# A long convolution inside a three-branch block: the real parts on VectorE, splits between the products, a place of its own for the odd frequencies

## The reference

```python
def fft_conv(u, cf):
    L = u.shape[1]
    U = jnp.fft.rfft(u.astype(jnp.float32), n=2 * L, axis=1)
    y = jnp.fft.irfft(U * cf[None], n=2 * L, axis=1)[:, :L]
    return y.astype(u.dtype)

z = x1 * (fft_conv(v, cf[:, 0]) + hy_d[0] * v)
z = x2 * (fft_conv(z, cf[:, 1]) + hy_d[1] * z)
```

## Time and profile before

| what | value |
|---|---|
| median of 3 runs | 1131.82 us |
| profiled execution | 1131.72 us |
| span of its trace | 1130.0 us |
| PE busy | 1078.3 us, 95% of the span |
| DVE busy | 726.5 us, 64% |
| ACT busy | 539.4 us, 48% |
| POOL busy | 74.9 us, 7% |

### The profile page before, as it was taken

The page is one execution under the profiler, slowest core; times in us unless marked ns, Lnnn a source line. Parts: engine busy times, 40 slices in busy tenths (PEclk is TensorE's granted clock), DMA queues, the critical chain, the costliest instruction groups (busy, mean ns, idle before and its releaser), DMA issues.

```text
span 1130.0 us, 14634 instructions
## 1 busy us (share of the span) xinstructions
PE 1078.3 (95%) x4942; PEld 869.9 (77%) x4942; DVE 726.5 (64%) x1187; ACT 539.4 (48%) x828; POOL 74.9 (7%) x70
## 2 busy tenths in 40 slices
PE   5999999999999999999999998899899999999998
PEld 4777678888887878788888777677577877888887
DVE  2865875554557987755455677987938676545553
ACT  3654454444445555644444462545346545444442
POOL 5013000000000100000000002201500000000000
PEclk9999999999999999999999999998899999999999
DMA  9454255656555534565655552443234445555553
GB/s 243 136 170 137 76 162 185 194 187 186 186 186 169 169 129 130 174 193 187 187 188 186 168 153 89 147 134 112 93 129 132 150 160 173 188 186 186 186 186 112
DMA packets 133599, 182.04 MB, mean 161 GB/s; under 512 B 11446, under 2 KB 80322, under 8 KB 133490
## 3 DMA queue, kind: packets, MB, share of 16 engines
q1 hardware_dynamic: 132266, 178.40, 50.2%
q0 software_dynamic: 1056, 2.57, 1.1%
q10 hardware_dynamic: 232, 0.49, 0.1%
HBM read 180.36 MB, written 1.05 MB: 161 GB/s over the span
## 4 chain that ended last, share of the span: by engine, by line
PE 75%; DVE 16%; ACT 5%; issue 2%; DMA 1%; SPq 1%; POOL 0%; DVEq 0%; ACTq 0%; POOLq 0%
PE ps L1788 14%; PE ps L1799 14%; PE ps L1791 14%; PE ps L1809 6%; PE ps L1810 6%; PE ps L1814 6%; DVE wlo L1042 5%; PE ps L1773 2%; PE ps L1775 2%; PE ps L1774 2%; DMA raw<-in_a_w_in 1%; PE ps L1879 1%; ACT whi L581 1%; PE ps L1862 1%; PE ps L2001 1%
## 5 line engine op out<-in xcount | busy, mean ns | idle before, releaser
L1042 DVE TENSOR_TENSOR wlo<-raw,whi 128x1024 fp32r<-128x1024 f32 x338 | 410.9, 1247 | 154.6 <-ACT whi L581 154.0
L581 ACT ACTIVATE whi<-raw 128x1024 fp32r<-128x1024 f32 x338 | 342.1, 1053 | 115.6 <-DMA raw<-in_a_w_in 28.1
L1788 PE MATMUL ps<-whi,ath 128*128 128x512 f32 (+1 forms) x896 | 360.7, 403 | 7.0 <-DVE atl L1056 4.8
L1791 PE MATMUL ps<-whi,atl 128*128 128x512 f32 (+1 forms) x896 | 351.8, 393 | 0.0
L1799 PE MATMUL ps<-wlo,ath 128*128 128x512 f32 (+1 forms) x896 | 243.0, 393 | 5.9 <-DVE wlo L1042 5.9
L1788 PEld LDWEIGHTS ps<-whi,ath 128*128 128x128 f32 x896 | 170.7, 191 | 51.9 <-issue 10.3
L1799 PEld LDWEIGHTS ps<-wlo,ath 128*128 128x128 f32 x896 | 168.7, 190 | 42.8 <-DVE wlo L1042 7.6
L1791 PEld LDWEIGHTS ps<-whi,atl 128*128 128x128 f32 x896 | 170.8, 191 | 33.6 <-issue 0.5
L1809 PE MATMUL ps<-whi,brh 128*128 128x512 f32 x272 | 106.5, 392 | 0.4 <-issue 0.4
L1810 PE MATMUL ps<-whi,brl 128*128 128x512 f32 x272 | 105.9, 389 | 0.0
L1118 DVE TENSOR_TENSOR brl<-ps,brh 128x512 fp32r<-128x512 f32 x33 | 22.8, 692 | 95.8 <-ACT brh L627 95.8
(11 more groups left out here) (338 smaller groups left out, 1043.8 us busy)
## 6 DMA issues: line engine op xcount, KB each, us to landing
raw<-in_ffn_w_in SPq DMA_DIRECT2D x176, 256.0 KB, 3.0
raw<-in_ffn_w SPq DMA_DIRECT2D x132, 256.0 KB, 2.9
raw<-in_w_in SPq DMA_DIRECT2D x104, 256.0 KB, 2.9
raw<-in_ffn_w_out SPq DMA_DIRECT2D x88, 256.0 KB, 2.8
raw<-in_a_w_in SPq DMA_DIRECT2D x48, 256.0 KB, 3.4
raw<-in_b_w_in SPq DMA_DIRECT2D x48, 256.0 KB, 3.1
raw<-in_a_w_out SPq DMA_DIRECT2D x16, 256.0 KB, 2.9
raw<-in_b_w_out SPq DMA_DIRECT2D x16, 256.0 KB, 2.9
```

The source lines that it names most:

```text
L581: a_(unit_view(whi, slot, w), unit_view(raw, slot, w), ACT.Copy).then_inc(hi_ready, 1)
L1042: v_.tensor_tensor(unit_view(wlo, slot, w), unit_view(raw, slot, w), unit_view(whi, slot, w), ALU.subtract).then_inc(lo_ready, 1)
L1788: mm(ps[bk + t][:, 0:w], ath[:, k, t * P:(t + 1) * P], rh[:, kk, :], start=k == 0, stop=False)
L1791: mm(ps[bk + t][:, 0:w], atl[:, k, t * P:(t + 1) * P], rh[:, kk, :], start=False, stop=False)
```

## The change

The real parts are made by DVE, in spectral_end, beside the imaginary ones, and POOL has no part in the round. The second pair of products gets a function of its own, spectral_imag, and one unit split stands ahead of it and one behind it, where two stood ahead of both. forward(o) signals after each pair of products, ACT copies the odd half of each pair as soon as that pair is signalled, and puts it in h_o, which overlaps no tile that is in use in the two rounds. DVE folds the first pair when its copy is there. The semaphore counts follow.

```diff
--- before.py
+++ after.py
@@ -307,6 +307,7 @@
         C_th = W(7680, 2048).rearrange("p (t n) -> p t n", t=NT)
         h_u = W(7680, 2048).rearrange("p (i n) -> p i n", i=4)
         C_mg = W(9728, 2048).rearrange("p (t n) -> p t n", t=NT)
+        h_o = W(11776, 1024).rearrange("p (i n) -> p i n", i=2)
         h_w = W(9728, 2048).rearrange("p (i n) -> p i n", i=4)
         C_qT = W(11776, 1024).rearrange("p (h t) -> p h t", h=4)
         C_kT = W(12800, 512).rearrange("p (h t) -> p h t", h=2)
@@ -508,17 +509,6 @@
                     nc.gpsimd.tensor_tensor(y, y, B_T1[:, kind, t, :].unsqueeze(1).to_broadcast([P, 4, BD]),
                                             ALU.mult).then_inc(sem("b_scaled"), 1)
 
-
-            def hyena_sums(o):
-
-                pool.wait_ge(sem("h_prod"), 6 * o + 2)
-                nc.gpsimd.tensor_tensor(h_w[:, 0:2, :], h_w[:, 0:2, :], h_w[:, 2:4, :], ALU.subtract).then_inc(sem("h_y"), 1)
-                pool.wait_ge(sem("h_y"), 3 * o + 1)
-                nc.gpsimd.tensor_tensor(h_w[:, 2, :], h_w[:, 0, :], h_w[:, 1, :], ALU.add).then_inc(sem("h_y"), 1)
-                nc.gpsimd.tensor_tensor(h_w[:, 3, :], h_w[:, 0, :], h_w[:, 1, :], ALU.subtract).then_inc(sem("h_y"), 1)
-
-            hyena_sums(0)
-            hyena_sums(1)
 
             pool.wait_ge(evac_act, ACT_EVACS[18])
             pool.wait_ge(sem("c_ssq"), 5)
@@ -860,9 +850,9 @@
 
             def h_odd(o):
 
-                act.wait_ge(sem("h_fwd"), o + 1)
                 for kind in range(2):
-                    a_(C_vt[:, kind, :], ps[5 + 2 * kind][:, :], ACT.Copy).then_inc(sem("h_odd"), 1)
+                    act.wait_ge(sem("h_fwd"), 2 * o + kind + 1)
+                    a_(h_o[:, kind, :], ps[5 + 2 * kind][:, :], ACT.Copy).then_inc(sem("h_odd"), 1)
 
             def c_squares(pieces):
 
@@ -1543,23 +1533,34 @@
 
             def spectral(o):
 
-                dve.wait_ge(sem("h_odd"), 2 * o + 2)
-                ec, oc, es, os = ps[4][:, :], C_vt[:, 0, :], ps[6][:, :], C_vt[:, 1, :]
-                for i, (a, b, op) in enumerate(((ec, oc, ALU.add), (ec, oc, ALU.subtract), (es, os, ALU.add), (os, es, ALU.subtract))):
-                    v_.tensor_tensor(h_u[:, i, :], a, b, op).then_inc(sem("h_folded"), 1)
+                for kind in range(2):
+                    dve.wait_ge(sem("h_odd"), 2 * o + kind + 1)
+                    even, odd = ps[4 + 2 * kind][:, :], h_o[:, kind, :]
+                    v_.tensor_tensor(h_u[:, 2 * kind, :], even, odd, ALU.add).then_inc(sem("h_folded"), 1)
+                    if kind == 0:
+                        v_.tensor_tensor(h_u[:, 1, :], even, odd, ALU.subtract).then_inc(sem("h_folded"), 1)
+                    else:
+                        v_.tensor_tensor(h_u[:, 3, :], odd, even, ALU.subtract).then_inc(sem("h_folded"), 1)
                 dve.wait_ge(sem("h_folded"), 4 * o + 4)
                 v_.tensor_tensor(h_w[:, 0:2, :], h_u[:, 0:2, :], H[:, o, 0:2, :], ALU.mult).then_inc(sem("h_prod"), 1)
                 v_.tensor_tensor(h_w[:, 2:4, :], h_u[:, 2:4, :], H[:, o, 2:4, :], ALU.mult).then_inc(sem("h_prod"), 1)
 
-            def spectral_end(o):
+            def spectral_imag(o):
 
                 dve.wait_ge(sem("h_prod"), 6 * o + 2)
                 v_.tensor_tensor(h_u[:, 0:2, :], h_u[:, 0:2, :], H[:, o, 2:4, :], ALU.mult).then_inc(sem("h_prod"), 1)
                 v_.tensor_tensor(h_u[:, 2:4, :], h_u[:, 2:4, :], H[:, o, 0:2, :], ALU.mult).then_inc(sem("h_prod"), 1)
+
+            def spectral_end(o):
+
                 dve.wait_ge(sem("h_prod"), 6 * o + 4)
-                link(v_.tensor_tensor(h_u[:, 0:2, :], h_u[:, 0:2, :], h_u[:, 2:4, :], ALU.add))
+                v_.tensor_tensor(h_w[:, 0:2, :], h_w[:, 0:2, :], h_w[:, 2:4, :], ALU.subtract).then_inc(sem("h_parts"), 1)
+                v_.tensor_tensor(h_u[:, 0:2, :], h_u[:, 0:2, :], h_u[:, 2:4, :], ALU.add).then_inc(sem("h_parts"), 1)
+                dve.wait_ge(sem("h_parts"), 2 * o + 2)
+                v_.tensor_tensor(h_w[:, 2, :], h_w[:, 0, :], h_w[:, 1, :], ALU.add).then_inc(sem("h_prod"), 1)
+                v_.tensor_tensor(h_w[:, 3, :], h_w[:, 0, :], h_w[:, 1, :], ALU.subtract).then_inc(sem("h_y"), 1)
                 v_.tensor_tensor(h_u[:, 2, :], h_u[:, 0, :], h_u[:, 1, :], ALU.subtract).then_inc(sem("h_prod"), 1)
-                v_.tensor_tensor(h_u[:, 3, :], h_u[:, 0, :], h_u[:, 1, :], ALU.add).then_inc(sem("h_prod"), 1)
+                v_.tensor_tensor(h_u[:, 3, :], h_u[:, 0, :], h_u[:, 1, :], ALU.add).then_inc(sem("h_y"), 1)
 
             def hyena_gate(o):
                 for m in range(4):
@@ -1578,6 +1579,8 @@
             h_taps(0)
             feed(U_C + 11)
             spectral(0)
+            feed(U_C + 12)
+            spectral_imag(0)
             feed(U_C + 13)
             spectral_end(0)
             feed(U_C + 15)
@@ -1586,6 +1589,8 @@
             hyena_gate(0)
             feed(U_C + 20)
             spectral(1)
+            feed(U_C + 21)
+            spectral_imag(1)
             feed(U_C + 22)
             spectral_end(1)
             feed(U_C + 24)
@@ -2241,11 +2246,13 @@
                 pe.wait_ge(sem("h_tok"), NT * (o + 1))
                 for i in range(4):
                     ins = mm(ps[4 + i][:, :], fwd[:, i, :], C_vt[:, i % 2, :], start=True, stop=True)
+                    if i == 1:
+                        ins.then_inc(sem("h_fwd"), 1)
                 ins.then_inc(sem("h_fwd"), 1)
 
             def backward(o):
 
-                pe.wait_ge(sem("h_y"), 3 * o + 3)
+                pe.wait_ge(sem("h_y"), 2 * o + 2)
                 pe.wait_ge(sem("h_prod"), 6 * o + 6)
                 for m in range(4):
                     for q in range(2):
```

## The result

The changed kernel takes 1125.78 us (median of 5 runs, 1122.50 to 1126.87) against 1133.38 us (5 runs, 1130.24 to 1134.98): ratio 0.9928, 95% interval 0.9905 to 0.9951. The forecast was 1124.3 us, 0.7% faster. The profiled execution took 1125.78 us.

What follows compares the result with a forecast made beforehand. Bound: PE waiting for DVE, itself held by POOL, and half clock. PE's 4.85 us lead after round 0, plus 0.5 and 2.05 in round 1, gives 7.4 (7.5 by schedule): 1131.82 to 1124.3 us, range 1122.6 to 1126.0.

Steps and rivals of the forecast that it cites:

- Folds earlier in round 0: Odd frequencies' own place, one count per pair: round 0's folds end 1.75 us earlier; round 1 gains 0.5 us.
- Less DVE a round: Each round DVE loses 4.4 us of POOL contention and gains 2.35 us of real parts: net 2.05 us less.
- Order of the splits: In each round, weight splits placed between the products: priced at 0, bounds -0.2 to +0.1 us.
- Round 0's wait gone, full clock behind it: Before round 0's backward transform PE's 3.16 us wait goes, 0.9 us in hand; full clock gives 1.7 us.
- Rival 1: Clock not given back in the backward transform, or a later wait newly loses its clock: 1126.0 us; chance 0.14.
- What is late next: Round 1's backward turn needs DVE's gate, ending about 693.8; PE arrives at 694.4, clear by 0.6 us.
- Unit 20 and unit 22: PE's waits for low weight parts in round 1: about 0.6 of 0.75 us goes; 2.8 of 4.88 us remain.
- Rival 2: Round 1's gain eaten by a late high part or DMA: 1127 to 1128.6 us; chance 0.06.
- Rival 3: DVE's slow rate comes from operands, not POOL, so its added work comes on top: 1134.1 us; chance 0.05.
- Clock later on: Clock behind the remaining wait for unit 22 and later waits: kept at 0, bounds -1.7 to +1.7 us.
- Rival 4: The stretch behind 763 also runs at full clock: 1122.6 us; chance 0.05.
- Does it last?: From 749.50 on, waits hang on PE, DVE and ACT alone, so the whole rest moves by 7.5 us.

Runs made afterwards that it cites:

- e4: Changed kernel with POOL also doing its old three instructions on memory nobody needs, no instruction of the two rounds waiting for them; ratio 1.0006.
- e5: Changed kernel with POOL starting three memsets, which only write, at the point of its old work; 1127.0 us in one run, ratio not timed.
- e3: Changed kernel with both weight splits of each round put back ahead of the imaginary products; 1124.62 us, ratio 0.9921 to the kernel before.
- e1: Changed kernel with odd frequencies copied over the tokens again, behind one signal for all four forward products; 1125.31 us, ratio 0.9930 to the kernel before.
- e6: Kernel before with only DVE making the real parts and POOL none; 1126.06 us, ratio 0.9951.
- e7: Kernel before with only the odd frequencies' own place, signals and folds per pair; POOL still makes the real parts; 1128.79 us, ratio 0.9977.
- e2: Changed kernel with POOL making the real parts again; 1131.01 us, ratio 0.9972 to the kernel before.
- e8: Changed kernel with the differential attention's query and key rotations and key scaling moved from POOL to DVE; 1114.96 us, ratio 0.9851 to the kernel before.

## Why the prediction was right

Step by step, with starts from the fixed point where two kernels are compared:

- *Folds earlier in round 0.* 1.75 us forecast; products start at 673.37 - 643.12 = 30.25 instead of 31.94 us: 1.69. In round 1 0.5 us was forecast: forward(1) starts 5.00 us earlier and the fold 5.49, so 0.49.
- *Less DVE a round.* 2.05 forecast; from the first product to the next split 13.78 us before (674.47 to 688.25) and 11.62 after (673.37 to 684.99): 2.16. The mechanism, POOL's instructions holding DVE, is shown by e4, where nothing in the rounds needs POOL, and e5 takes instructions that only write out of it.
- *Order of the splits.* 0 forecast; 0.13 (e3).
- *Round 0's wait gone, full clock behind it.* 0.9 us in hand forecast, 0.7 measured (last half ends at 685.07, PE starts at 685.75). The 1.7 us of clock came back. Rival 1 is out.
- *What is late next.* The gate ends at 694.37 ahead of PE's 694.82: 0.45 in hand, 0.6 forecast.
- *Unit 20 and unit 22.* Waits of 0.1 and 2.8 us forecast, 0.27 and 2.70 measured. Rival 2 is out.
- *Rival 3*, DVE slow by its operands, is out: the same products take 1.22 us.
- *Clock later on.* Priced at 0 with bounds of 1.7 us either way. Rival 4 (the stretch behind 763 at full clock) came true in part: the low clock there lasted half as long, worth 1.25 us.
- *Does it last?* Here the text was wrong in one sentence. It said that from 749.50 on "all waits hang on PE, DVE and ACT alone". POOL's rotations hold DVE at 792 us, and PE's longest remaining wait hangs on how they fall. The lead of 7.64 us came; 2.3 us went in that place, 1.25 came from the clock, and 1.05 net was lost.

The forecast of the lead at the turn is borne out step by step. That the medians fit as well (7.6 us apart, 7.5 forecast) is in part luck: the interval of the ratio allows 5.6 to 10.8 us, the two traced executions differ by 5.9 us, and two effects that the sum had at 0 have opposite signs.

How far is that loss the change's? e5 runs as the changed kernel up to the rotations and had a wait of 4.88 us; e1, e6 and e7 had 4.83 to 4.87; e2 and e3 7.20 and 7.16, e4 7.87. One profile each can't say how often each outcome comes in a kernel. In all nine the two starts, of POOL's first multiply and of the 128x2 add, lie within 0.01 us of each other; in the five kernels with the short wait (before among them) the add took 0.16 us, in the four with the long one 1.27 or 1.28. What decides between the two stays open, so the 2.3 us can't be put down to the change. That the turns of POOL and DVE there are the cause of PE's wait is shown by e8.

## What to carry to other kernels

When an instruction doubles in the middle of a list, look at what GpSimd does at that time before looking at its operands: work moved from GpSimd to VectorE can shorten VectorE's own list (here 2.35 us added, 4.4 us freed a round). Look for every stretch where both engines read SBUF, not only the one under edit: the second one (e8, 9.1 us of the tail) was worth no less than the first (7.64 us at the turn). Parts that shorten the same wait don't add up, since the wait and the clock behind it can come back only once.

## What the runs showed of the hardware that was not expected

- Waits of PE of 0.41, 1.12, 1.35 and 1.48 us ahead of the first backward transform all kept full clock (3.81 to 3.84 us); 3.16 us cost 1.7 and 3.60 us cost 2.9 us. The wait of 1.71 to 1.73 us further on (ahead of 763.03 before, of 755.99 in the changed kernel) was followed by low clock about 1 us later before and about 2 us later in the changed kernel, and by none in e2, e4 and e6, which have 1.00 from there to the next wait for DVE some 24 us on. The 2.70 us wait for unit 22 was followed by low clock 1 us later in the changed kernel (from about 720.4); e6, with 2.82 us there, has 1.00 from 721 to 745 us. So the length of a wait alone didn't tell whether the clock would fall.
- Small instructions are held as well: a 128x2 add on DVE took 1.28 instead of 0.16 us. So are tensor_scalar instructions: one of 128x32 with a single input took 2.37 us in the changed kernel (787.37) and 0.18 in e8, and two of 128x256 took 3.53 us together and 0.62 when free.
- One and the same GpSimd instruction, the 128x1024 add of the rotations, took 3.26 us for the first token half and 2.34 for the second in the changed kernel. Which part of that is waiting for DVE was not measured.
